# Transposing the queries and keys of an attention block with VectorE blocks and DMAs instead of TensorE

## Chip, core and metric

The kernel runs on one NeuronCore of one Trainium2 chip. The metric is device time in microseconds (us) of one execution of the whole program; the median of the runs is compared. A NeuronCore has five engines with instruction streams of their own: TensorE (PE, matrix products, its weight loads shown as PEld), VectorE (DVE), ScalarE (ACT), GpSimd (POOL) and SyncE (SP, which issues DMAs). They wait for one another through semaphores only.

## What is computed

A decoder trunk of two layers on 256 tokens of width 1024, in float32. Each layer is a mixer sub-layer (three branches in parallel, merged by gates) and a feed-forward sub-layer. Cut to what matters here:

```
z = rms_norm(x) @ w_in
c_q, c_kv, k_r, u_conv, u_pool, gate_logits = split(z)
q = (rms_norm(c_q) @ w_uq).reshape(B, S, 8, 64 + 32)     # 8 heads; the last 32 columns get rotary
k_nope = (rms_norm(c_kv) @ w_uk).reshape(B, S, 8, 64);  k_rope = rotary(k_r)   # shared by the heads
v = (rms_norm(c_kv) @ w_uv).reshape(B, S, 8, 64)
o = softmax(causal((q_nope @ k_nope.T + q_rope @ k_rope.T) / sqrt(96))) @ v    # per head
y_attn = o @ w_attn_o;  y_conv = ...;  y_pool = ...
x = x + rms_norm((g0 * y_attn + g1 * y_conv + g2 * y_pool) @ w_mix_o)
x = x + rms_norm((silu(h @ w_gate) * (h @ w_up)) @ w_down)      # h = rms_norm(x)
```

## The kernel before

**Weights as a stream of units.** The weights of a layer are cut into 135 units of at most 128x1024 numbers. SP loads unit after unit into a ring of five buffers (`raw`). Matrix products are made in a split precision: ScalarE writes a rounded copy of each unit (`w_hi`, L858), VectorE writes the rest (`w_lo = raw - w_hi`, L1185 and L1189), and TensorE makes three products for one (L438 to L440: high by high, high by low, low by high). A ring buffer is given back when TensorE has used its unit, so ScalarE and VectorE can be at most five units ahead of TensorE. One unit of a `col_group` is twelve matmuls of 512 columns.

**Order of work.** The instruction order of every engine is written by hand. TensorE goes through the groups G, A, CQ, CKV, Q, POOL, K (one unit, number 23), V (unit 24), then 24 units of gate logits (25 to 48), then the output products. Attention is threaded between the gate units: after gate unit `i` with `i` even, TensorE does `scores(i/2 - 1)`, the transposes of the probabilities of the step before, and the weighted values of the one before that (`after_gate`). So `scores(0)` stands behind the third gate unit (`i` = 2). There are 8 steps: 4 pairs of heads by 2 halves of the tokens.

**Queries and keys.** A score product wants queries and keys with the 96 dimensions of a head on the partitions. They come out of the projections with tokens on the partitions, in `q_sb` and `k_sb`. TensorE turns them with `transposes` (L512): a group is four heads of one half of the tokens, 4 transposes into one PSUM buffer `tp`, and ScalarE copies it to SBUF (`store_T`, L997) into `q_t` (in `gates`) and `k_t` (in `u_sb` and `hc`). Per layer there are 4 groups Q0 to Q3 and 4 groups K0 to K3: Q0, Q1 ahead of the K unit, Q2, Q3 ahead of the V unit (behind eight `band` matmuls of the pooling branch, L679 and L681), K0, K1 behind gate unit `i` = 0, K2, K3 behind `i` = 1. Each score product is one `pe.matmul` per head (L719), with 128 keys for the first half of the tokens and 256 for the second; the profile shows a float32 `pe.matmul` as two records.

**VectorE around it.** After the rotary of q (`rope`, L1242 to L1249) VectorE does unit 23, three convolution taps (L1264), unit 24, the rotary of k, three taps, and then `lo(u)` and three taps for each of the units 25 to 28. In the gate loop it does for each `i` the attention work (mask and maximum L1372 and L1375), `lo(29 + i)` and four taps. It does the 124 taps of a layer in one fixed order.

**GpSimd.** It computes the inverse norms (L1578, L1581) and rests from the one of c_kv until the sums over the convolution (`tile_sum`, L1625), which wait for the last tap.

**A path that exists already.** In the feed-forward sub-layer the hidden activations are transposed without TensorE: VectorE transposes 32x32 blocks (`turn`, L1488), and SP moves the blocks to their partitions with 16 DMAs a chunk (`place`, L405).

Of the kernel before, what the change touches and what calls it, by code (L numbers as in the profile page):

```python
# [44 lines left out]

BLK = 32
QUADS = P // BLK


POOL_LO = {(l, u) for l in range(LAYERS) for u in (U_FFN, U_FFN + 1)}  # L50
# [35 lines left out]
def fulls(pair, use):  # L86
# [2 lines left out]

TP = (["X0", "X1", "X2", "X3", "HC0", "HC1", "CQ0", "CQ1", "CKV0", "CKV1", "Q0", "Q1", "Q2", "Q3", "K0", "K1", "K2", "K3",
       "MT0", "MT1", *(f"{piece}{n}" for n in range(8) for piece in "PV"), "O0", "O1",
       "M0", "M1", "M2", "M3", "F0", "F1", "F2", "F3"])
TPN = {name: n for n, name in enumerate(TP)}
T_USES = len(TP)
HI_OF = [n for n in TP if n[:2] != "HC" and n[0] not in "PQKV"]
MUL_OF = [n for n in TP if n[0] in "XF"]


# [48 lines left out]
def build(nc, W, pool_w, par_d, const_d, gain_d, x_d, xc_d, pos_d, out_d):  # L149
    with ExitStack() as ctx:  # L150
        def sb(name, shape, dt=F32):
            return ctx.enter_context(nc.sbuf_tensor(name, shape, dt))

        def sem(name):
            return ctx.enter_context(nc.semaphore(name))
# [10 lines left out]
        gain = sb("gain", [P, D])  # L166
        const = sb("const", [P, NCONST])
        par = sb("par", [P, LAYERS, NPAR])
        hc = sb("hc", [P, TOK, CONV])
        sg = sb("sg", [P, TOK, 512])  # L170
        u_sb = sb("u_sb", [P, TOK, 512])
        hcT = sb("hcT", [P, CT, TAPS - 1 + SEQ])
        cacc = sb("cacc", [P, CT, SEQ])
        gates = sb("gates", [P, TOK, 3 * D])
# [24 lines left out]
        o_sb = qk_flat[:, 2048:3072].rearrange("p (t n) -> p t n", t=TOK)  # L199
        junk = qk_flat[:, 0:D]  # L200
        pooled = sg[:, :, :].rearrange("p t n -> p (t n)").rearrange("p (g n) -> p g n", g=4)


        q_t = [gates[:, hh, 2 * D:3 * D].rearrange("p (h s) -> p h s", h=4) for hh in range(2)]
        k_t = [buf[:, :, :].rearrange("p t n -> p (t n)").rearrange("p (h s) -> p h s", h=4)
               for buf in (u_sb, hc)]
        rope_a, rope_b = hc[:, 0, :], hc[:, 1, :]
        xc = hc[:, :, :].rearrange("p t n -> p (t n)").rearrange("p (c n) -> p c n", c=CT)
        sq = sg[:, :, :].rearrange("p t n -> p (t n)").rearrange("p (c n) -> p c n", c=CT)
# [62 lines left out]
        q_roped = sem("q_roped")  # L272
        k_roped = sem("k_roped")
        k_nope = sem("k_nope")
        conv_dve = sem("conv_dve")
        csum_done = sem("csum_done")
        centred = sem("centred")
# [157 lines left out]
        def _(pe):  # L435
# [23 lines left out]
            for l in range(LAYERS):  # L459
# [47 lines left out]
                def transposes(n, blocks):  # L507

                    b = n % 2
                    tp_wait(n)  # L510
                    for i, (src, rows) in enumerate(blocks):
                        mm = pe.transpose(tp[0:rows, b, i * P:(i + 1) * P], src, ident)  # L512
                    mm.then_inc(tp_full[b], 1)
# [140 lines left out]

                col_group(U_POOL, 4, 2, 512, 1, "POOL", XT)

                def q_transposes(hh):
                    for t in range(TOK):
                        if hh == 0:
                            pe.wait_ge(q_roped, l + 1)  # L660
                        transposes(TPN["Q0"] + 2 * hh + t, [(q_sb[:, t, h * QK:(h + 1) * QK], QK)
                                                            for h in range(4 * hh, 4 * hh + 4)])

                q_transposes(0)

                for t in range(TOK):
                    tp_emptied(pe, l, TPN["CKV0"] + t)
                col_group(U_K, 1, 2, 512, 0, "K", HT, kt0=H_CKV)
# [5 lines left out]
                for h in range(2):  # L674
# [6 lines left out]
                        mm = pe.matmul(misc[:, h, c + P:c + SEQ], u_sb[:, 1, g * P:(g + 1) * P],  # L681
                                       band[:, SEQ:BANDW], start=False, stop=True)
                    mm.then_inc(misc_full[h], 1)
                q_transposes(1)

                col_group(U_V, 1, 2, 512, 1, "V", HT, kt0=H_CKV)

# [8 lines left out]
                                           pw_sb[:, g * P:(g + 1) * P], pooled[:, g, :], start=True, stop=True)  # L696
                        mm.then_inc(tp_full[n % 2], 1)

                def k_transposes(n):
                    hh, t = n // 2, n % 2  # L700
                    if hh == 0:
                        pe.wait_ge(k_roped, l + 1)
                        pe.wait_ge(k_nope, l * TOK + (t + 1))
                    transposes(TPN["K0"] + n, [(k_sb[:, t, h * QK:(h + 1) * QK], QK)
                                               for h in range(4 * hh, 4 * hh + 4)])

                def scores(n):
                    hp, t = n // 2, n % 2
                    keys = (t + 1) * P
                    if n == 0 or n == 4:  # L710
                        for k in range(2):
                            tp_emptied(pe, l, TPN["K0"] + n // 2 + k)
                    if n < 2:
                        misc_emptied(pe, l, n, M_D)
                    else:
                        pe.wait_ge(exp_done, l * STEPS + n - 1)
                    for i in range(2):
                        h = 2 * hp + i
                        mm = pe.matmul(misc[:, n % 2, i * keys:(i + 1) * keys], q_t[h // 4][0:QK, h % 4, tokens(t)],  # L719
                                       k_t[h // 4][0:QK, h % 4, 0:keys], start=True, stop=True)  # L720
                    mm.then_inc(s_done, 1)

                def p_transposes(n):
# [27 lines left out]
                              ).then_inc(misc_full[0], 1)  # L751

                def attention(i):
                    if i < 2:
                        for n in range(TOK):
                            k_transposes(2 * i + n)
                    s_n, p_n, v_n = after_gate(i)
                    if s_n is not None:
                        scores(s_n)
                    if p_n is not None:  # L760
                        p_transposes(p_n)
                    if v_n is not None:
                        weighted_values(v_n)
                    if i in O_AFTER:
                        o_transposes(O_AFTER.index(i))
                    if i == MT_AFTER:
                        pool_products()
                    if i == MEAN_AFTER:
                        norm_mean()
# [72 lines left out]
        def _(act):  # L842
# [3 lines left out]
            for l in range(LAYERS):  # L846
# [143 lines left out]
                    act.activation(u_sb[:, t, :], acc[:, 2 + t, :], ACT.Copy,  # L990
                                   scale=rstd(l, R_X + t)).then_inc(free[2 + t], 1)

                def store_T(name, dst):

                    n = TPN[name]
                    tp_filled(act, l, n)
                    act.activation(dst, split3(tp[0:QK, n % 2, :], 4), ACT.Copy).then_inc(tp_free[n % 2], 1)  # L997

                def store_q(hh):
                    for t in range(TOK):  # L1000
                        store_T(f"Q{2 * hh + t}", q_t[hh][0:QK, :, tokens(t)])

                store_q(0)
                his(26, 27)
                for t in range(TOK):
                    bank(t, "K")
# [6 lines left out]
                for h in range(2):  # L1013
                    act.wait_ge(misc_full[h], l * 2 + 1)
                    act.activation(pooled[:, 2 * h:2 * h + 2, :], split3(misc[:, h, :], 2),
                                   ACT.Copy).then_inc(misc_free[h], 1)
                store_q(1)
                his(27, 28)
                for t in range(TOK):
                    bank(2 + t, "V")  # L1020
# [37 lines left out]
                for i in range(GATES):  # L1058
                    if i == MEAN_AFTER + 1:
                        conv_square()  # L1060
                    hi(U_GATE + 4 + i)
                    j = i // 4
                    if i == 3:
                        act.wait_ge(rhalf_done, (l + 1) * TOK)
                    if i % 4 == 3:
                        pair, branch, h = j % 2, j // 2, j % 2
                        for t in range(TOK):
                            bank(2 * pair + t, f"GATE{j}")
                            act.activation(gates[:, t, branch * D + 512 * h:branch * D + 512 * (h + 1)],
                                           acc[:, 2 * pair + t, :], ACT.Tanh,  # L1070
                                           scale=rhalf[:, l * TOK + t:l * TOK + t + 1]
                                           ).then_inc(free[2 * pair + t], 1)
                    if i < 2:
                        for n in range(2 * i, 2 * i + 2):
                            store_T(f"K{n}", k_t[i][0:QK, :, tokens(n % 2)])
                    s_n, p_n, _ = after_gate(i)
                    if p_n is not None:
                        store_p(p_n)
                    if s_n is not None:
                        exponentials(s_n)  # L1080
                    if i in O_AFTER:
                        half_ = O_AFTER.index(i)
                        hi_T(f"O{half_}", hT_hi[:, H_O + 2 * half_:H_O + 2 * half_ + 2, :])
                    if i == MT_AFTER:
                        for h in range(2):
                            hi_T(f"MT{h}", hT_hi[:, H_POOL + 2 * h:H_POOL + 2 * h + 2, :])
                    if i == 18:
                        act.preload_act_table(ACT.Silu)
# [61 lines left out]
        def _(dve):  # L1150
# [23 lines left out]
            for l in range(LAYERS):  # L1174
# [142 lines left out]
                    misc_emptied(dve, l, t, M_Q)  # L1317
                qr = q_sb[:, :, :].rearrange("p t (h d) -> p t h d", h=HEADS)[:, :, :, NOPE:QK]
                rope(qr, qr).then_inc(q_roped, 1)
                los(23, 24)  # L1320
                taps(3)
                los(24, 25)
                for t in range(TOK):
                    acc_freed(dve, l, 2 + t, "CKV")
# [2 lines left out]
                rope(k_sb[:, :, :].rearrange("p t (h d) -> p t h d", h=HEADS)[:, :, :, NOPE:QK],  # L1327
                     cq[:, :, k0:k0 + ROPE].unsqueeze(2)).then_inc(k_roped, 1)
                taps(3)
                for u in range(25, 29):  # L1330
                    lo(u)
                    taps(3)

                def conv_centre():

# [203 lines left out]
        def _(pool):  # L1539
# [30 lines left out]
            for l in range(LAYERS):  # L1570
# [48 lines left out]
                norm(R_CKV)  # L1619
                norm(R_CKV + 1)  # L1620

                def tile_sum(src, which):

                    halves = cprod[:, :, :]
                    pool.tensor_tensor(halves, src[:, 0:2, :], src[:, 2:4, :], ALU.add).then_inc(csum_done, 1)  # L1625
                    pool.wait_ge(csum_done, l * 4 + 2 * which + 1)
                    pool.tensor_tensor(csum[:, which, :], cprod[:, 0, :], cprod[:, 1, :], ALU.add
                                       ).then_inc(csum_done, 1)
# [136 lines left out]
```

## Time and profile before

| | us |
|---|---|
| median of 3 runs (lowest to highest) | 794.12 (794.04 to 794.16) |
| the profiled execution's own time | 794.23 |
| its span, first to last instruction | 792.4 |

| engine | busy share of the span |
|---|---|
| TensorE | 99% |
| VectorE | 72% |
| ScalarE | 54% |
| GpSimd | 10% |

The busy share is an average over the span. Matmuls are pipelined, so the time of one record is longer than the distance to the next; where a stretch of TensorE is priced, the distance from start to start counts. Start times in the rows are us from the first instruction.

### The profile page before, as it was taken

The numbers are of one execution on the slowest core, as the hardware profiler recorded it, in microseconds if no ns is written. First come the engines' busy times: TensorE is split into PE (matmuls) and PEld (weight loads), VectorE is DVE, ScalarE is ACT, GpSimd is POOL, SyncE is SP. The second block draws the span as 40 slices with busy tenths as digits, with TensorE's granted clock in tenths as the row PEclk, the third lists the DMA queues.
The fourth block names the chain that finished last, engine by engine and source line by source line (L and its number), as shares of the span: only waits on it lengthen the run. The fifth ranks groups of instructions, "written<-read, shape, count | busy, mean of one in ns | idle before, by whom it ended". The sixth has DMA issues, their size and how long they took to land.

```text
span 792.4 us, 10213 instructions
## 1 busy us (share of the span) xinstructions
PE 784.0 (99%) x3740; PEld 661.7 (84%) x3740; DVE 567.6 (72%) x814; ACT 427.6 (54%) x604; POOL 78.2 (10%) x111
## 2 busy tenths in 40 slices
PE   8999999999999999999999999999999999999997
PEld 7998888888888888888889888888888888888885
DVE  6688999879675666654476979996896755556553
ACT  6577565564564454454475666556545545445441
POOL 1620000113210000000221100002203000000000
PEclk9999999999999999999999999999999999999999
DMA  9675444536567666676355654444564676666641
GB/s 357 225 247 164 156 160 134 185 125 192 171 234 229 215 210 207 210 249 208 130 201 170 223 176 133 145 150 160 166 213 167 228 223 210 226 208 213 208 156 54
DMA packets 51729, 151.26 MB, mean 191 GB/s; under 512 B 9776, under 2 KB 14896, under 8 KB 51680
## 3 DMA queue, kind: packets, MB, share of 16 engines
q1 hardware_dynamic: 51280, 148.93, 56.6%
q0 software_dynamic: 256, 1.16, 0.4%
q8 instruction: 30, 0.49, 0.3%
q10 hardware_dynamic: 144, 0.52, 0.2%
q14 instruction: 19, 0.16, 0.1%
HBM read 143.77 MB, written 1.05 MB: 183 GB/s over the span
## 4 chain that ended last, share of the span: by engine, by line
PE 98%; DMA 1%; ACT 0%; DVE 0%; DVEq 0%; POOLq 0%; issue 0%; SPq 0%; POOL 0%; ACTq 0%
PE acc L438 28%; PE acc L440 28%; PE acc L439 28%; PE acc L557 7%; PE tp L512 3%; PE misc L719 1%; PE tp L737 1%; PE tp L524 1%; DMA gates<-x_cols 1%; PE misc L679 0%; PE tp L695 0%; PE misc L439 0%; PE misc L438 0%; PE misc L440 0%; PE misc L681 0%; ACT w_hi L858 0%
## 5 line engine op out<-in xcount | busy, mean ns | idle before, releaser
L1189 DVE TENSOR_TENSOR w_lo<-raw,w_hi 128x1024 fp32r<-128x1024 f32 (+2 forms) x246 | 299.1, 1227 | 128.3 <-ACT w_hi L858 127.6
L858 ACT ACTIVATE w_hi<-raw 128x1024 fp32r<-128x1024 f32 (+2 forms) x252 | 258.6, 1039 | 167.6 <-PE acc L440 161.1
L438 PE MATMUL acc<-w_hi,xT_hi 128*128 128x512 f32 (+2 forms) x692 | 268.2, 388 | 0.0
L440 PE MATMUL acc<-w_hi,xT_lo 128*128 128x512 f32 (+2 forms) x692 | 264.9, 383 | 0.0
L439 PE MATMUL acc<-w_lo,xT_hi 128*128 128x512 f32 (+2 forms) x692 | 264.7, 383 | 0.0
L440 PEld LDWEIGHTS acc<-w_hi,xT_lo 128*128 128x128 f32 x692 | 129.9, 188 | 24.8
L439 PEld LDWEIGHTS acc<-w_lo,xT_hi 128*128 128x128 f32 x692 | 130.0, 188 | 23.9
L438 PEld LDWEIGHTS acc<-w_hi,xT_hi 128*128 128x128 f32 x692 | 130.0, 188 | 23.6
L438 PE MATMUL acc<-w_hi,hT_hi 128*128 128x512 f32 (+1 forms) x300 | 117.3, 391 | 0.0
L440 PE MATMUL acc<-w_hi,hT_lo 128*128 128x512 f32 (+1 forms) x300 | 116.2, 387 | 0.0
L439 PE MATMUL acc<-w_lo,hT_hi 128*128 128x512 f32 (+1 forms) x300 | 116.1, 387 | 0.0
L1264 DVE SCALAR_TENSOR_TENSOR cacc<-hcT,par,cacc 128x256 f32<-128x256 f32 x240 | 101.3, 480 | 0.0
L440 PEld LDWEIGHTS acc<-w_hi,hT_lo 128*128 128x128 f32 x300 | 56.3, 188 | 11.4
L439 PEld LDWEIGHTS acc<-w_lo,hT_hi 128*128 128x128 f32 x300 | 56.4, 188 | 11.0
L438 PEld LDWEIGHTS acc<-w_hi,hT_hi 128*128 128x128 f32 x300 | 56.3, 188 | 10.9
L1578 POOL TENSOR_SCALAR mean<-ssq 128x1 f32<-128x1 f32 x23 | 8.8, 383 | 443.8 <-ACT qk L877 443.3
L1185 DVE SCALAR_TENSOR_TENSOR w_lo<-raw,par,w_hi 128x512 fp32r<-128x512 f32 (+1 forms) x30 | 24.9, 864 | 6.4 <-ACT w_hi L858 6.4
L1165 DVE TENSOR_TENSOR acc<-acc,gain 128x512 f32<-128x512 f32 x16 | 10.4, 691 | 25.6 <-ACT qk L877 22.6
L1495 DVE TENSOR_TENSOR hT_lo<-gates,hT_hi 128x512 fp32r<-128x512 f32 (+1 forms) x24 | 14.4, 640 | 19.6 <-ACT hT_hi L1105 19.6
L1045 ACT ACTIVATE qk<-tp 128x256 f32<-128x256 f32 (+1 forms) x16 | 7.9, 491 | 36.2 <-PE tp L512 36.2
L1105 ACT ACTIVATE hT_hi<-gates 128x512 fp32r<-128x512 f32 (+1 forms) x24 | 13.0, 587 | 24.8 <-DMA gates<-gates 24.8
L557 PE MATMUL acc<-w_hi,xT_hi 128*128 128x512 f32 x76 | 24.0, 397 | 1.6 <-ACT w_hi L858 1.6
(147 smaller groups left out, 638.9 us busy)
## 6 DMA issues: line engine op xcount, KB each, us to landing
raw<-weights SPq DMA_DIRECT2D x247, 512.0 KB, 3.7
raw<-weights SPq DMA_DIRECT2D x14, 384.0 KB, 3.8
gates<-gates SPq DMA_DIRECT2D x160, 32.0 KB, 2.5
raw<-weights SPq DMA_DIRECT2D x8, 288.0 KB, 4.1
gain<-gains SPq DMA_DIRECT2D x4, 512.0 KB, 6.4
x_sb<-x_rows SPq DMA_DIRECT2D x2, 512.0 KB, 9.5
out_rows<-x_sb SPq DMA_DIRECT2D x4, 256.0 KB, 2.0
const<-consts POOLq DMA_DIRECT2D x1, 896.0 KB, 7.9
```

What stands on the lines that cost most here:

```text
L438: pe.matmul(out, a_hi, b_hi, start=start, stop=False)
L439: pe.matmul(out, a_hi, b_lo, start=False, stop=False)
L440: return pe.matmul(out, a_lo, b_hi, start=False, stop=stop)
L512: mm = pe.transpose(tp[0:rows, b, i * P:(i + 1) * P], src, ident)
L557: mm = pe.matmul(b, src[:, kt, tokens(t)], w[:, s, 512 * j:512 * (j + 1)], start=kt == 0 and src is xT_hi and w is w_hi, stop=last and kt ...
L858: ins = act.activation(w_hi[:, s, first:end], raw[:, s, first:end], ACT.Copy, scale=by)
L1105: act.activation(hid_part(hT_hi, j, t), placed_for(j, t), ACT.Copy).then_inc(hid_hi, 1)
L1165: dve.tensor_tensor(acc[:, 2 * t + h, :], acc[:, 2 * t + h, :], gain[:, k], ALU.mult).then_inc(yg_done, 1)
L1185: ins = dve.scalar_tensor_tensor(out=w_lo[:, s, first:end], in0=raw[:, s, first:end], scalar=par[:, l, col:col + 1], in1=f(w_hi[:, s, firs ...
L1189: ins = dve.tensor_tensor(w_lo[:, s, 0:width], raw[:, s, 0:width], f(w_hi[:, s, 0:width]), ALU.subtract)
L1264: ins = dve.scalar_tensor_tensor(out=cacc[:, c, :], in0=src, scalar=w, in1=cacc[:, c, :], op0=ALU.mult, op1=ALU.add)
L1495: dve.tensor_tensor(hid_part(hT_lo, j, t), placed_for(j, t), f(hid_part(hT_hi, j, t)), ALU.subtract).then_inc(hid_lo, 1)
```

## The change

Queries and keys are no longer transposed by TensorE. VectorE transposes them in 32x32 blocks, three instructions for q and three for k (one for each 32 of the 96 dimensions of a head, over all heads and tokens). GpSimd's queue then issues 12 DMAs for q and 12 for k, each of 32 partitions by 512 numbers (64 KB, SBUF to SBUF), which bring block column `c` of token block `q` to partitions `32c` to `32c+31`. The keys are used where they land (`u_hc`, a joint buffer of what were `u_sb` and `hc`), in four runs of 32 columns for 128 keys; the queries land in four buffers and ScalarE copies them into `q_t` (`store_q`, 4 copies of 96x512 in place of the 8 copies of `store_T`). `scores(0)` waits for all of it. Score products over 256 keys become two of 128. VectorE's taps move: three ahead of the V unit fall away there, and the units 27 and 28 get five each.

```diff
-TP = ([... "CKV0", "CKV1", "Q0", "Q1", "Q2", "Q3", "K0", "K1", "K2", "K3",
+TP = ([... "CKV0", "CKV1",
...
+        turned_q = [gates[:, i // 2, 512 * (i % 2):512 * (i % 2 + 1)] for i in range(QK // BLK)]
+        turned_k = [gates[:, 0, D:D + 512], gates[:, 1, D:D + 512], gates[:, 0, D + 512:2 * D]]
+        placed_q = [qk_flat[:, 512 * i:512 * (i + 1)] for i in range(QUADS - 1)] + [gates[:, 1, 512:1024]]
...
@@ TensorE: q_transposes and k_transposes and their calls fall away
                 def scores(n):
-                    if n == 0 or n == 4:
-                        for k in range(2):
-                            tp_emptied(pe, l, TPN["K0"] + n // 2 + k)
+                    if n == 0:
+                        pe.wait_ge(q_stored, QUADS * (l + 1))
+                        pe.wait_ge(k_in, 16 * HEAD_MOVES * (l + 1))
...
                         h = 2 * hp + i
-                        mm = pe.matmul(misc[:, n % 2, i * keys:(i + 1) * keys], q_t[h // 4][0:QK, h % 4, tokens(t)],
-                                       k_t[h // 4][0:QK, h % 4, 0:keys], start=True, stop=True)
+                        for k in range(t + 1):
+                            mm = pe.matmul(misc[:, n % 2, i * keys + k * P:i * keys + (k + 1) * P],
+                                           q_t[0:QK, t, h, :], k_t[0:QK, :, k, h, :], start=True, stop=True)
...
@@ ScalarE: store_T and store_q(0), store_q(1) of the old form fall away
+                def store_q(q):
+                    act.wait_ge(q_in, 16 * HEAD_MOVES * (l + 1))
+                    src = placed_q[q][0:QK, :].rearrange("p (t h j) -> p t h j", t=TOK, h=HEADS)
+                    act.activation(q_t[0:QK, :, :, q * BLK:(q + 1) * BLK], src, ACT.Copy).then_inc(q_stored, 1)
...
                     if i < 2:
-                        for n in range(2 * i, 2 * i + 2):
-                            store_T(f"K{n}", k_t[i][0:QK, :, tokens(n % 2)])
+                        store_q(2 * i)
+                        store_q(2 * i + 1)
...
@@ VectorE
+                def turn_heads(src, dst, done):
+                    v = src[:, :, :].rearrange("p t (h d) -> p t h d", h=HEADS)
+                    for c in range(QK // BLK):
+                        dve.transpose(dst[c].rearrange("p (t h j) -> p t h j", t=TOK, h=HEADS),
+                                      v[:, :, :, c * BLK:(c + 1) * BLK]).then_inc(done, 1)
                 los(23, 24)
-                taps(3)
+                dve.wait_ge(q_roped, l + 1)
+                turn_heads(q_sb, turned_q, q_turned)
                 los(24, 25)
...
                 taps(3)
-                for u in range(25, 29):
+                los(25, 26)
+                taps(3)
+                los(26, 27)
+                taps(2)
+                dve.wait_ge(k_roped, l + 1)
+                dve.wait_ge(k_nope, (l + 1) * TOK)
+                turn_heads(k_sb, turned_k, k_turned)
+                for u in range(27, 29):
                     lo(u)
-                    taps(3)
+                    taps(5)
...
@@ GpSimd, behind the four norms of c_q and c_kv
+                def move_heads(src, dst, turned_, landed):
+                    pool.wait_ge(turned_, (l + 1) * (QK // BLK))
+                    for c in range(QK // BLK):
+                        for q in range(QUADS):
+                            pool.dma_start(dst(slice(BLK * c, BLK * (c + 1)), q), src[c][BLK * q:BLK * (q + 1), :]
+                                           ).then_inc(landed, 16)
+                move_heads(turned_q, lambda p, q: placed_q[q][p, :], q_turned, q_in)
+                for h in range(2):
+                    pool.wait_ge(misc_full[h], l * 2 + 1)
+                move_heads(turned_k, lambda p, q: u_hc[p, q // 2, q % 2, :], k_turned, k_in)
```

## Rows read from the trace of the kernel before

**Rows 1.** The page's busy times (us, share, instructions) and granted clock, in 40 slices.
```profile
PE 784.0 (99%) x3740; PEld 661.7 (84%) x3740; DVE 567.6 (72%) x814; ACT 427.6 (54%) x604; POOL 78.2 (10%) x111
...
PEclk9999999999999999999999999999999999999999
```

**Rows 2.** Waits of TensorE: us in total, times, longest.
```profile
PE acc L557 <- ACT w_hi L858: 1.6, 1, 1.6
```

**Rows 3.** Groups by form: count, then busy us, mean ns of one.
```profile
L512 PE MATMUL tp<-const,qk 128*96 128x128 f32 x64 | 8.3, 272 | 0.0
```

**Rows 4.** Timeline of TensorE in both layers: start us, us, what.
```profile
64.57 0.40 PE L440 MATMUL acc<-w_hi,xT_lo 128*128 128x512 f32 x1
64.80 1.04 PE L512 MATMUL tp<-const,qk 128*96 128x128 f32 x8
65.60 0.48 PE L438 MATMUL acc<-w_hi,hT_hi 128*128 128x512 f32 x1
65.91 0.39 PE L439 MATMUL acc<-w_lo,hT_hi 128*128 128x512 f32 x1
...
74.67 0.39 PE L438 MATMUL acc<-w_hi,xT_hi 128*128 128x512 f32 x1
...
77.39 1.03 PE L512 MATMUL tp<-const,qk 128*96 128x128 f32 x8
...
84.64 0.61 PE L719 MATMUL misc<-u_sb,gates 96*128 96x128 f32 x4
85.09 1.89 PE L695 MATMUL tp<-sg,pw_sb 128*128 128x256 f32 x8
...
92.28 1.03 PE L719 MATMUL misc<-u_sb,gates 96*128 96x256 f32 x4
93.15 0.38 PE L512 MATMUL tp<-const,qk 128*128 128x128 f32 x2
...
474.30 0.61 PE L719 MATMUL misc<-u_sb,gates 96*128 96x128 f32 x4
```

**Rows 5.** Timeline of VectorE, at the rotary in both layers and at a transpose.
```profile
61.39 1.41 DVE L1185 SCALAR_TENSOR_TENSOR w_lo<-raw,par,w_hi 128x512 fp32r<-128x512 f32 x2
62.71 1.27 DVE L1264 SCALAR_TENSOR_TENSOR cacc<-hcT,par,cacc 128x256 f32<-128x256 f32 x3
63.91 1.41 DVE L1185 SCALAR_TENSOR_TENSOR w_lo<-raw,par,w_hi 128x512 fp32r<-128x512 f32 x2
...
67.48 1.22 DVE L1189 TENSOR_TENSOR w_lo<-raw,w_hi 128x1024 fp32r<-128x1024 f32 x1
68.62 1.27 DVE L1264 SCALAR_TENSOR_TENSOR cacc<-hcT,par,cacc 128x256 f32<-128x256 f32 x3
...
284.35 1.30 DVE L1488 STREAM_TRANSPOSE gates<-u_sb 128x512 f32<-128x512 f32 x2
...
449.87 1.41 DVE L1185 SCALAR_TENSOR_TENSOR w_lo<-raw,par,w_hi 128x512 fp32r<-128x512 f32 x2
```

**Rows 6.** Timeline of ScalarE.
```profile
68.63 0.69 ACT L1007 ACTIVATE qk<-acc,rstd 128x512 f32<-128x512 f32 x1 [0.45 <-PE acc L440]
...
78.03 1.08 ACT L997 ACTIVATE u_sb<-tp 96x512 f32<-96x512 f32 x2 [0.57 <-PE tp L512]
```

**Rows 7.** Timeline of GpSimd and, last row, of VectorE.
```profile
16.62 0.81 POOL L1595 DMA_DIRECT2D const<-consts  x1 [15.80 <-ACT w_hi L858]
17.43 0.56 POOL L1596 DMA_DIRECT2D pos_i<-pos  x1
...
20.84 0.62 POOL L1599 DMA_DIRECT2D par<-params  x1
21.47 0.53 POOL L1600 DMA_DIRECT2D const<-consts  x1
...
52.69 1.09 POOL L1578 TENSOR_SCALAR mean<-ssq 128x1 f32<-128x1 f32 x1
...
20.76 2.36 DVE L1189 TENSOR_TENSOR w_lo<-raw,w_hi 128x1024 fp32r<-128x1024 f32 x2 [0.30 <-ACT w_hi L858]
```

**Rows 8.** DMA issues: count, KB each, median us from issue to landing.
```profile
gates<-gates SPq DMA_DIRECT2D x160, 32.0 KB, 2.5
par<-params POOLq DMA_DIRECT2D x1, 161.0 KB, 3.9
```

More of the change, by code:

```diff
@@ L47 @@
 QUADS = P // BLK
+HEAD_MOVES = QUADS * (QK // BLK)
 POOL_LO = {(l, u) for l in range(LAYERS) for u in (U_FFN, U_FFN + 1)}
@@ L88, in fulls @@
     return len([u for u in upto if pair == 0 or u not in WIDE])
-TP = (["X0", "X1", "X2", "X3", "HC0", "HC1", "CQ0", "CQ1", "CKV0", "CKV1", "Q0", "Q1", "Q2", "Q3", "K0", "K1", "K2", "K3",
+TP = (["X0", "X1", "X2", "X3", "HC0", "HC1", "CQ0", "CQ1", "CKV0", "CKV1",
        "MT0", "MT1", *(f"{piece}{n}" for n in range(8) for piece in "PV"), "O0", "O1",
@@ L96 @@
 T_USES = len(TP)
-HI_OF = [n for n in TP if n[:2] != "HC" and n[0] not in "PQKV"]
+HI_OF = [n for n in TP if n[:2] != "HC" and n[0] not in "PV"]
 MUL_OF = [n for n in TP if n[0] in "XF"]
@@ L168, in build @@
         par = sb("par", [P, LAYERS, NPAR])
-        hc = sb("hc", [P, TOK, CONV])
         sg = sb("sg", [P, TOK, 512])
-        u_sb = sb("u_sb", [P, TOK, 512])
+        u_hc = sb("u_hc", [P, 2, TOK, 512])
         hcT = sb("hcT", [P, CT, TAPS - 1 + SEQ])
@@ L201, in build @@
         pooled = sg[:, :, :].rearrange("p t n -> p (t n)").rearrange("p (g n) -> p g n", g=4)
-        q_t = [gates[:, hh, 2 * D:3 * D].rearrange("p (h s) -> p h s", h=4) for hh in range(2)]
-        k_t = [buf[:, :, :].rearrange("p t n -> p (t n)").rearrange("p (h s) -> p h s", h=4)
-               for buf in (u_sb, hc)]
+        u_sb, hc = u_hc[:, 0], u_hc[:, 1]
+        q_t = gates[:, :, 2 * D:3 * D].rearrange("p t (h s) -> p t h s", h=HEADS)
+        k_t = u_hc[:, :, :, :].rearrange("p b c (t h j) -> p (b c) t h j", t=TOK, h=HEADS)
+        turned_q = [gates[:, i // 2, 512 * (i % 2):512 * (i % 2 + 1)] for i in range(QK // BLK)]
+        turned_k = [gates[:, 0, D:D + 512], gates[:, 1, D:D + 512], gates[:, 0, D + 512:2 * D]]
+        placed_q = [qk_flat[:, 512 * i:512 * (i + 1)] for i in range(QUADS - 1)] + [gates[:, 1, 512:1024]]
         rope_a, rope_b = hc[:, 0, :], hc[:, 1, :]
@@ L274, in build @@
         k_nope = sem("k_nope")
+        q_turned = sem("q_turned")
+        k_turned = sem("k_turned")
+        q_in = sem("q_in")
+        q_stored = sem("q_stored")
+        k_in = sem("k_in")
         conv_dve = sem("conv_dve")
@@ L655, in _ @@
                 col_group(U_POOL, 4, 2, 512, 1, "POOL", XT)
[L657 to L664, printed above, removed]
                 for t in range(TOK):
@@ L683, in _ @@
                     mm.then_inc(misc_full[h], 1)
-                q_transposes(1)
                 col_group(U_V, 1, 2, 512, 1, "V", HT, kt0=H_CKV)
@@ L697, in pool_products @@
                         mm.then_inc(tp_full[n % 2], 1)
[L699 to L705, printed above, removed]
                 def scores(n):
@@ L753, in attention @@
                 def attention(i):
-                    if i < 2:
-                        for n in range(TOK):
-                            k_transposes(2 * i + n)
                     s_n, p_n, v_n = after_gate(i)
@@ L991, in _ @@
                                    scale=rstd(l, R_X + t)).then_inc(free[2 + t], 1)
[L993 to L1003, printed above, removed]
+                def store_q(q):
+                    act.wait_ge(q_in, 16 * HEAD_MOVES * (l + 1))
+                    src = placed_q[q][0:QK, :].rearrange("p (t h j) -> p t h j", t=TOK, h=HEADS)
+                    act.activation(q_t[0:QK, :, :, q * BLK:(q + 1) * BLK], src, ACT.Copy).then_inc(q_stored, 1)
                 his(26, 27)
@@ L1016, in _ @@
                                    ACT.Copy).then_inc(misc_free[h], 1)
-                store_q(1)
                 his(27, 28)
```

## The prediction

> **What bounds the kernel now.** I read the busy times first: TensorE is busy 99% of the span [rows 1]. The waits of TensorE then show one pause of 1.6 us, at the start, and nothing behind it [rows 2]. So every instruction taken from TensorE shortens the kernel by its distance to the next one, as long as nothing new keeps TensorE waiting; and every new wait counts in full. The other engines have room on average, but what counts is when the new chain VectorE, GpSimd, DMA, TensorE ends in two places, at `scores(0)` of each layer. The timelines of those stretches decide it.
>
> **What goes.** The transposes of q and k are 64 matmuls of the form 128*96 [rows 3]: 32 a layer, in four lots of eight. The lot at 64.80 ends when the next matmul starts at 65.60, and that one takes 0.31 us to its successor where 0.23 is the rule (64.57 to 64.80) [rows 4]: 0.80 + 0.08 = 0.88 us. Four lots are 3.5 us a layer, 7.0 in all. On ScalarE eight copies of 96x512 become four; a pair takes 1.08 us [rows 6] and the cost is nothing either way, since they lie beside TensorE's gate units.
>
> **What costs TensorE nothing or almost.** A score step over 256 keys takes 0.87 us for four records (92.28 to 93.15), one over 128 keys 0.45 for four (84.64 to 85.09) [rows 4]. Eight records of 128 are then 0.9, as before. Keys read in four runs of 32 have no row; bounds are nothing and, if every one of the 96 records that read keys (64 of them in the second halves) cost double, 96 x 0.11 = 10.6 us. I take nothing, since the products that read a plain run are the nearest.
>
> **When the keys are turned.** In layer 0 VectorE starts unit 23 at 61.39, with q already rotated. From there, start to start [rows 5]: unit 23 1.32 (61.39 to 62.71); three transposes of q; unit 24, the rotary of k and three taps 3.57 (63.91 to 67.48); unit 25 1.14 (67.48 to 68.62); three taps 1.19 (62.71 to 63.91); unit 26 1.14; two taps 0.80; three transposes of k. Two transposes of 128x512 take 1.30 us; with one at 0.69 that is one each 0.61, so three are 1.83. (The new ones read runs of 32 numbers at a stride of 96; the 20 old ones also pick blocks, so I take their price.) Sum: 12.8, and 0.1 for the semaphore: k is turned at 74.3, q at 64.6. ScalarE's copy of the keys, at 68.63 before [rows 6] and earlier now, isn't late. In layer 1 VectorE starts the same unit at 449.87, so q is turned at 453.1 and k at 462.8.
>
> **The train of DMAs.** Four issues on GpSimd's queue took 0.81, 0.56, 0.62 and 0.53 us [rows 7], whatever their size. I take 0.57, the mean of the last three. The twelve of q end at 64.6 + 6.8 = 71.4, ahead of the keys: hidden. The last of the keys is issued at 74.3 + 11 x 0.57 = 80.6. From issue to landing SP's copies inside SBUF take 2.5 us, GpSimd's load of 161 KB 3.9, but this with the DMA engines full [rows 8]. I take 3.5, nearer to GpSimd's own; bounds 2.5 and 3.9. The keys are in at 84.1 in layer 0 and at 462.8 + 6.3 + 3.5 = 472.6 in layer 1.
>
> The Trainium skill ("DMA: Bandwidth & Descriptors", Specifications) puts the first byte of a DMA issued from GpSimd at about 1 us and one from SP at about 0.6. By that the landing would be 2.5 + 0.4 = 2.9 us, an estimate from that page, and the sum below would end 1.2 us lower. No row here has a small GpSimd copy on idle DMA engines.
>
> **When TensorE comes.** `scores(0)` started at 84.64 and 474.30 [rows 4]. All four lots stood ahead of it: 81.1 and 470.8. So TensorE waits 3.0 us in layer 0 and 1.8 in layer 1; I add 0.2 each for the refill. The copies of q by ScalarE aren't last: q lands at 64.6 + 11 x 0.57 + 3.5 = 74.4, ScalarE comes to them about 76 (two copies stood at 78.03 [rows 6]) and the second pair follows one unit later, by 79. Behind it nothing waits longer: the waiting TensorE has ScalarE's and VectorE's units up to the ring's end.
>
> **VectorE's debt.** It gets 6 transposes, 3.7 us a layer, and TensorE asks 0.5 to 2 us earlier. At `i` = 2 VectorE comes to the mask of step 0 about 86, 1 us later against the scores than before. A gate unit needs its `w_lo` four units (4 x 2.72 us, 74.67 to 77.39 being one [rows 4]) after VectorE may start on it, and the probabilities have two gate units to be ready; both cover that debt. Without the cover (VectorE 8 us late) it would stall TensorE for the excess.
>
> **Sum.** -7.0 + 3.0 + 1.8 + 0.4 = -1.8. The profiled execution took 794.23, 0.11 above the median, so 792.4 there and **792.3** as median. Bounds of this case: issues of 0.53 and landing in 2.5 give waits of 1.5 and 0.3, sum -4.8, 789.3; issues of 0.63 (mean of all four) and landing in 3.9 give 4.1 and 2.9, sum +0.4, 794.5.
>
> **Rivals.**
>
> *The train is slow, the kernel slower.* An issue costs more than 0.57: the first row is 0.81, and a GpSimd operation on a single column took 1.09 us at 52.69, in a stretch where VectorE was working. VectorE is busy nearly without a break here. Against it: the issues at 20.84 and 21.47 lay inside two such operations (20.76 to 23.1) and took 0.62 and 0.53 [rows 7]. Each 0.1 us more adds 2 x 11 x 0.1 = 2.2; the sum is zero at 0.65 us an issue, and above that the change loses. At 0.81, q's train ends just as k is turned (74.3): -1.8 + 22 x 0.24 = +3.5, 797.6. At 1.09 q's train holds the keys up too (until 77.7; layer 1 466.2): waits 12.1 and 10.9, sum +16.4, 810.5. The Trainium skill ("SBUF — State Buffer", on the shared port pair) has the rule: GpSimd can't write descriptors while VectorE runs an operation in a two-port mode, but a `tensor_tensor` takes only the read side. By that the train isn't held, as rows 7 say; by its copy rule it would be, and no row here shows a copy.
>
> *No wait at all, the full gain.* The keys would have to land by 81.1, that is 6.8 us after being turned for 11 issues and a landing. With issues of 0.53 that leaves 1.0 for the landing, below every row. The time would be 787.1. For it speaks only that issues may overlap.
>
> *The pause costs clock.* Granted clock was full (2.4 GHz) throughout [rows 1], also over the only pause, 1.6 us [rows 2]; no row tells of 3 us. If it fell to half in each layer for one gate unit (2.72 us): +5.4, sum +3.6, 797.7. The Trainium skill ("TensorE: Matmul & The Clock Gate", Why this matters for your kernels) warns of pauses of this kind between bursts of matmuls.
>
> *Keys in runs slow the products.* +10.6 at most, sum +8.8, 802.9. No row speaks for it or against it.
>
> **Chances.** Forecast 0.47; slow train 0.33; full gain 0.07; clock 0.08; runs 0.05. A measurement here can tell about 0.2%, 1.6 us. Faster by more (below 792.5): half of the forecast, 0.25, and the full gain, with some issues below the rows: 0.37. Within: most of the rest of the forecast and the mild end of the slow train, 0.23. Slower: 0.40. The range for 8 in 10 leaves out the full gain and a train above about 0.9 us an issue (each 0.1 past 0.81 adds 2 x 2.3, as both trains count): 789 to 802; the forecast's own range is 789.3 to 794.5.
>
> **What would show it.** L512 with 128*96 gone, TensorE busy 7 us less. 24 issues a layer on GpSimd at about 0.57 us from 64.6 and from 74.3, the last landing about 84. One wait of TensorE at L719 on a DMA in each layer, 3.0 and 1.8 us: longer if the train is slow, absent if the full gain is had. Matmuls behind the wait at 0.23 us a step; 0.45 would be the clock. Six transposes of 0.69 us a layer. The prediction is wrong if the issues take more than 0.65 us or a landing much more than 3.9.

## The result, and the profile after

| | us |
|---|---|
| before, median of 5 runs (lowest to highest) | 794.12 (793.93 to 794.16) |
| changed, median of 5 runs | 796.84 (796.31 to 801.25) |
| ratio, 95% interval | 1.0051 (1.0028 to 1.0073) |
| profiled execution of the changed kernel, its span | 796.84, 795.0 |

The changed kernel is slower by 2.7 us, where 1.8 us less was forecast. Its runs also spread over 4.9 us, those of before over 0.2. The ratio is that of the means (798.12 to 794.07), which the two longest runs lift; that of the medians is 1.0034. The page's busy times and granted clock after:

```profile
PE 779.8 (98%) x3708; PEld 658.3 (83%) x3708; DVE 574.3 (72%) x826; ACT 423.8 (53%) x596; POOL 102.8 (13%) x159
...
PEclk9999999999999999999999999999999999999999
```

TensorE's busy time fell by 4.2 us only [rows 1]. Its waits after (us in total, times, longest):

```profile
PE misc L712 <- issue: 6.8, 2, 4.1
PE misc L467 <- DVE diag L1135: 1.2, 1, 1.2
PE acc L567 <- ACT w_hi L848: 0.9, 1, 0.9
```

There are two new pauses ahead of the first scores of a layer (L712 is the score product, L719 before). "issue" stands there because the profile names no instruction that released them. The only things waited for there are the stored queries and the keys' DMAs; ScalarE had stored the last queries by 79.4 us, so it was the DMAs, and experiment 1 confirms it. The other two rows are pauses in the first 9 us, and stood there before as well. The chain that ended last, in order of time, around the two places (start, us, what):

```profile
80.92 0.23 PE acc L450
81.15 4.08 issue
85.23 1.18 PE misc L712 x4
86.41 2.90 PE tp L695 x8
89.31 0.23 PE acc L448
...
473.07 0.23 PE acc L450
473.30 2.76 issue
476.06 0.68 PE misc L712 x4
476.74 1.73 PE tp L695 x8
478.47 0.23 PE acc L448
```

TensorE arrives at 81.15, as forecast (81.1), and waits 4.08 us, then 2.76 us in layer 1. Behind the first pause the same work takes longer than behind the second: 4.08 us for the scores and the pooling products against 2.41. The windows show the clock in that stretch (columns: us, busy time and count by engine, granted clock, DMA share, GB/s):

```profile
78.00:81.00 3.00, 3.00 (x14) 2.26 (x13) 3.00 (x7) 2.35 (x4) 2.58 (x6) 1.00 1.05 249
81.00:85.00 4.00, 0.15 (x1) 0.00 (x0) 4.00 (x9) 0.00 (x0) 0.00 (x0) 1.00 1.02 264
85.00:87.00 2.00, 1.77 (x6) 1.68 (x7) 1.31 (x4) 0.00 (x0) 0.00 (x0) 0.56 0.90 311
87.00:89.00 2.00, 2.00 (x8) 1.61 (x6) 1.69 (x3) 1.38 (x5) 0.00 (x0) 0.59 0.02 6
...
474.00:476.00 2.00, 0.00 (x0) 0.00 (x0) 2.00 (x5) 0.00 (x0) 0.00 (x0) 1.00 0.87 252
476.00:478.00 2.00, 1.94 (x11) 1.81 (x12) 1.97 (x5) 0.29 (x2) 0.00 (x0) 1.00 0.82 268
```

Two things are to be seen. After the pause of 4.08 us the granted clock is at half (1.2 GHz) for some 3.4 us (the means of 0.56 and 0.59 over 4 us); after 2.76 us it stays full. And the DMA engines are full from 78 to 85 us, at only 249 and 264 GB/s, where the full engines moved 399 to 422 GB/s in the trace of before (4 to 16 us). The timeline of GpSimd, whose instructions here are the issues of the copies:

```profile
64.84 1.62 POOL L1626 DMA_DIRECT2D qk<-gates  x3 [10.36 <-DVE gates L1308]
...
70.34 0.50 POOL L1626 DMA_DIRECT2D gates<-gates  x1
74.73 5.85 POOL L1626 DMA_DIRECT2D u_hc<-gates  x12 [3.89 <-DVE gates L1308]
```

The train of the keys is quicker than forecast: 5.85 us for twelve, 0.49 each (0.57 forecast). Its last copy is issued at 80.1. The lines of the copies (ns of one issue, least, median, most) and of the landing in `u_hc`:

```profile
L1626 POOL DMA_DIRECT2D u_hc<-gates x24: 496/496/498, 74.7 to 471.1; - x24
...
DMA to landing us min/median/max: 1.8/4.0/5.1
```

From 80.1 to 85.2, when TensorE goes on, are 5.1 us. So the issue is not what is slow, the landing is. VectorE's part came as priced, 12 transposes of 0.69 us; so did the score steps over 256 keys, 0.89 us for eight records of 128:

```profile
94.78 0.89 PE misc L712 x8
...
L1308 DVE STREAM_TRANSPOSE gates<-qk 128x512 f32<-128x512 f32 x12 | 7.6, 685 | 0.0
```

The sum of the profiled executions (796.84 - 794.23 = +2.6): -7.0 for the transposes, +6.8 for the pauses, +1.7 for the clock (scores 85.23 to 86.20 in place of 0.45 us, pooling products 86.20 to 88.96 in place of 1.54 [rows 4]), +0.6 behind VectorE's last entry in the chain (see the last section), and 0.5 left over, which I put down to refills of TensorE and small shifts without having traced it.

```profile
85.23 1.18 PE L712 MATMUL misc<-u_hc,gates 96*128 96x128 f32 x4 [4.08 <-issue]
86.20 3.11 PE L695 MATMUL tp<-sg,pw_sb 128*128 128x256 f32 x8
88.96 0.58 PE L448 MATMUL acc<-w_hi,xT_hi 128*128 128x512 f32 x1
```

### The profile page after: what moved, and what is told of

Same layout as the page of the kernel before. It is cut to its first block, busy times and chain, and to the rows that moved or that the text cites. A ratio compares the mean times of both kernels' runs of the same rounds, so it can differ in the third digit from the quotient of the medians.

```text
span 795.0 us, 10195 instructions
## 1 busy us (share of the span) xinstructions
PE 779.8 (98%) x3708; PEld 658.3 (83%) x3708; DVE 574.3 (72%) x826; ACT 423.8 (53%) x596; POOL 102.8 (13%) x159
## 3 DMA queue, kind: packets, MB, share of 16 engines
HBM read 143.77 MB, written 1.05 MB: 182 GB/s over the span
## 4 chain that ended last, share of the span: by engine, by line
PE 97%; issue 1%; DMA 1%; ACT 0%; DVE 0%; DVEq 0%; POOLq 0%; SPq 0%; POOL 0%; ACTq 0%
PE acc L448 28%; PE acc L450 28%; PE acc L449 28%; PE acc L567 7%; PE tp L522 2%; PE misc L712 1%; PE tp L730 1%; PE tp L534 1%; DMA gates<-x_cols 1%; PE tp L695 1%; PE misc L680 0%; PE misc L450 0%; PE misc L449 0%; PE misc L448 0%; PE misc L682 0%
```

## Experiments

All times are medians; each ratio is that of the means, to the kernel before, run on the same chip. The edits are against the changed kernel and cut to what matters; `...` marks a cut.

**1. No copies: what are the transposes worth?**

```diff
-                        pe.wait_ge(k_in, 16 * HEAD_MOVES * (l + 1))
...
-                    act.wait_ge(q_in, 16 * HEAD_MOVES * (l + 1))
...
-                move_heads(turned_q, ...)                      # GpSimd: both trains left out
...
-                move_heads(turned_k, ...)
...
+            pool.memset(gates[:, 1, 512:1024], 0.0)            # once, so that the buffer holds numbers
```

> Leaves out all 48 copies between partitions and the waits on their landing (the scores then use what lies in the buffers; one buffer is set to zero once at the start); VectorE's six transposes and ScalarE's four copies a layer stay. Theory A (the 64 matmuls are worth 7.0 us, and the loss comes only from waiting for the landing and what the wait brings): no wait at the first scores, granted clock 0.999, 787.1 us. Rival B (VectorE's new work or the split score products cost TensorE time too): 788.5 or more. The stores at the end took 0.6 us longer in the two runs with GpSimd copies looked at; if that comes from the copies it is gone here, else it adds up to 0.7.

Measured: 787.59 us, ratio 0.9915 (0.9901 to 0.9928); runs within 0.2 us. There is no pause at the first scores; layer 0:

```profile
81.23 0.45 PE misc L711 x4
```

So leaving out the 64 matmuls is worth 6.7 us (794.27 before on this chip), and VectorE's transposes, ScalarE's copies and the split score products together cost at most the 0.3 us that are missing to 7.0. Theory A holds. All of the loss is in the copies.

**2. Weight loads held back while the keys travel.**

```diff
                 for u in range(0 if l else 1, UNITS):
+                    if u == 32:
+                        sp.wait_ge(k_in, 16 * HEAD_MOVES * (l + 1))
                     load(l, u, unit_width(u))
```

> The changed kernel with SP's load of weight unit 32 (and so of all behind it) held until the keys have landed, in each layer; TensorE needs that unit some 15 us later. Theory E (the last copies land 5 us after their issue because copies and weight loads together fill the DMA engines): the last landing falls to 3.5 us or less, the waits from 4.1 and 2.8 to about 2.6 and 1.3, the clock stays full, 794.1 - 7.0 + 3.9 + 0.2 = 791 to 792.5. Rival F (the landing time is GpSimd's own and doesn't depend on the loads): landing and waits as before, 796 to 797.

Measured: 789.1 us (789.08 to 789.4), ratio 0.9937 (0.9925 to 0.9949). This one wait (two lines) turns a loss of 2.7 us into a gain of 5.1. Landing in `u_hc` and the chain in layer 0:

```profile
DMA to landing us min/median/max: 1.8/1.9/2.2
...
81.16 0.86 issue
82.01 0.68 PE misc L714 x4
```

The train is the same (0.50 us an issue, from 74.7), but a copy lands in 1.9 us in place of 4.0. The pause is 0.86 us in layer 0 and gone in layer 1, less than theory E said, since it allowed 3.5 us for the landing; the time is below its 791 to 792.5 for the same reason. Theory E holds, F falls. The queues' packets, MB and shares of the 16 DMA engines from 78 to 81 us, with loads held:

```profile
q0 software_dynamic: 191, 0.39, 60.6%
```

and in the changed kernel:

```profile
q0 software_dynamic: 219, 0.46, 67.5%
q1 hardware_dynamic: 87, 0.29, 37.6%
```

and before, from 78 to 84 us, where the weight loads were alone:

```profile
q1 hardware_dynamic: 298, 1.09, 58.2%
```

Six copies were issued in those 3 us: 0.606 x 3 / 6 = 0.30 us of all engines for 64 KB. At one copy in 0.5 us the train alone takes 0.6 of the engines, and the weight loads took 0.58 of them in this place before. Together that is more than there is, so copies queue up behind loads, up to 5 us. A copy itself holds the engines no longer beside the loads than without them (0.675 x 3 us for 0.46 MB, 4.4 us per MB, against 0.606 x 3 for 0.39, 4.7): it waits for its turn and isn't moved more slowly. But per MB a copy costs more than a load (0.582 x 6 us for 1.09 MB, 3.2), which is a part of why the full engines move so little.

The mean shares explain only a part of the size: 0.18 too much over the 5.9 us of the train leaves 1.1 us of work behind, and the landing grew by 2.1 us in the median and 2.9 at most (from 1.9 and 2.2 to 4.0 and 5.1). The engines had been full from 70 to 74 us already (share 1.05), with the last copies of the queries beside the loads, and a load comes as one piece of 512 KB, by the figure above 1.7 us of all engines, an estimate. How much each of these adds wasn't separated.

**3. Keys turned earlier.**

```diff
-                taps(3)
                 los(25, 26)
                 taps(3)
-                los(26, 27)
-                taps(2)
                 dve.wait_ge(k_roped, l + 1)
                 dve.wait_ge(k_nope, (l + 1) * TOK)
                 turn_heads(k_sb, turned_k, k_turned)
+                los(26, 27)
+                taps(5)
```

> The changed kernel with VectorE's three transposes of the keys moved ahead of unit 26 and of three taps: they end about 3.1 us earlier (74.1 to about 71). GpSimd's train for the queries ends at 70.8, so the keys' train starts about 71.2 in place of 74.7, 3.5 us earlier. Theory A (the moment of the turn sets the wait): waits fall from 4.1 and 2.8 to about 0.6 and 0, the clock stays full, 794.1 - 7.0 + 0.6 + 0.2 = 787.9, at most 789.5. Rival B (the landing of the last copy is set by the DMA engines being full until then and doesn't move with the issue): waits stay above 2, 791 to 795.

Measured: 794.38 us, but from 791.28 to 801.78 over 12 runs; ratio 1.0015 (0.9993 to 1.0036). Neither expectation is met alone. The two long waits are 2.45 us in layer 0 and 1.04 in layer 1. The train starts 2.95 us earlier (71.78), TensorE goes on only 1.46 us earlier (83.77): half of the head start is lost again to the landing, whose median is 4.4 us, the longest 6.5. B is nearer. And the clock fell after the pause of only 2.45 us (not after that of 1.04):

```profile
DMA to landing us min/median/max: 3.5/4.4/6.5
...
81.32 2.45 issue
83.77 1.19 PE misc L712 x4
84.96 2.90 PE tp L695 x8
...
85.00:87.00 2.00, 2.00 (x6) 1.55 (x6) 1.97 (x6) 0.20 (x1) 0.00 (x0) 0.50 0.70 248
```

The mean clock of the runs goes with their time: 0.997 to 0.999 in those of 791.3 and 792.5 us, 0.992 and 0.990 in those of 800.0 and 801.8.

**4. The pause filled with work.**

```diff
                     if n == 0:
+                        misc_emptied(pe, l, 0, M_D)
+                        for _ in range(5):        # 3 in the second kernel
+                            pe.matmul(misc[:, 0, 0:512], ident, const[:, K_BAND:K_BAND + 512], start=True, stop=True)
                         pe.wait_ge(q_stored, QUADS * (l + 1))
                         pe.wait_ge(k_in, 16 * HEAD_MOVES * (l + 1))
```

> The changed kernel with five extra matmuls of 512 columns (ten records, about 2.1 us, result overwritten) ahead of TensorE's wait for queries and keys, in each layer: they fit into the pauses of 4.1 and 2.8 us and leave 2.0 and 0.7 of them. Theory C (the pause itself lets the clock fall, which costs 1.7 us in the profiled run and more in the runs of 799 and 801): 795.1 us, granted clock 0.999, and a spread below 0.5 us. Rival D (the low clock in that stretch has another cause than the pause): 796 to 801 as before, granted clock 0.99 to 0.996.

Measured: 796.98 us (796.51 to 797.95), ratio 1.0038 (1.0026 to 1.005), granted clock 0.998 to 0.999 in all five runs. The clock did what theory C said; the time (795.1 expected) and the spread (1.4 us in place of 0.5) didn't. Layer 0:

```profile
81.58 4.29 PE misc L705 x10
85.87 0.58 issue
```

The ten records take 4.29 us, double of what I allowed, and in layer 1 (pause 2.76) they hold TensorE up by 1.5 us themselves. So with three matmuls again:

> The changed kernel with three extra matmuls of 512 columns (six records of 0.43 us as measured with five of them, 2.6 us in all) ahead of the wait, in each layer; they fit into the pauses of 4.1 and 2.8 us. Theory C (the pause lets the clock fall): granted clock 0.999, 796.8 less 1.7 = 795.1, spread below 1 us. Rival D (another cause): 796 to 801 and clock 0.990 to 0.996 as in the changed kernel.

Measured: 795.25 us, ratio 1.0013 (1.0004 to 1.0022). Ten of eleven runs lie between 794.48 and 795.57 with a clock of 0.998 or 0.999; one is at 798.2 with 0.996, so the spread is 3.7 us where below 1 was expected. The chain in layer 0 and layer 1:

```profile
81.09 2.58 PE misc L705 x6
83.66 1.48 issue
85.14 0.68 PE misc L715 x4
85.83 1.73 PE tp L695 x8
...
471.60 2.58 PE misc L705 x6
474.18 0.51 issue
474.69 0.68 PE misc L715 x4
```

The keys come as late as in the changed kernel, but the work behind them takes 2.4 us, not 4.1. So 1.6 us of the loss, and most of the spread, come from the clock, and the clock falls when TensorE stands still: the same kernel with work in the pause keeps 0.998 or more in 15 of 16 runs. Theory C holds. The one run at 0.996 may be a fall after the 1.5 us of pause that was left; it wasn't profiled, so that isn't shown.

**5. Keys issued by SP.**

```diff
+                    if u == 32:                                # in SP's stream, ahead of the load
+                        sp.wait_ge(k_turned, (l + 1) * (QK // BLK))
+                        for h in range(2):
+                            sp.wait_ge(misc_full[h], l * 2 + 1)
+                        for c in range(QK // BLK):
+                            for q in range(QUADS):
+                                sp.dma_start(u_hc[BLK * c:BLK * (c + 1), q // 2, q % 2, :],
+                                             turned_k[c][BLK * q:BLK * (q + 1), :]).then_inc(k_in, 16)
...
-                move_heads(turned_k, ...)                      # GpSimd: the keys' train left out
```

> The changed kernel with the 12 copies of the keys issued by SP, ahead of its load of unit 32, in place of GpSimd. SP issues in order, so the loads behind stand back as in the kernel with held loads. SP's own copies take 0.6 us an issue, so the train is 7.2 us in place of 5.9. Theory E (what matters is that the loads stand back): landing 2 us after the last issue at 74.7 + 11 x 0.6 = 81.3, so 83.3, wait 2.1 in layer 0 and about 0.9 in layer 1, 790.5 to 792 us, clock seldom below full. Rival H (GpSimd's queue is at fault for the late landing, in whatever company): landing and waits clearly shorter than with held loads and GpSimd (0.9 and 0), below 789.1.

Measured: 792.48 us (790.79 to 792.75), ratio 0.9969 (0.9959 to 0.9979). SP's train, the chain in layer 0, and the granted clock behind the pause:

```profile
74.22 7.57 SPq L425 DMA_DIRECT2D u_hc<-gates  x12
...
81.19 2.10 issue
83.29 0.68 PE misc L720 x4
...
85.00:87.00 2.00, 2.00 (x6) 1.60 (x5) 1.97 (x6) 0.33 (x2) 0.00 (x0) 0.50 0.97 358
```

SP's issues take 0.63 us, GpSimd's 0.49; the landing is 2.0 us here and 1.9 with GpSimd and held loads. With the loads standing back both queues land alike, so GpSimd's queue isn't at fault and H falls; it is in fact the better one for this train. With the longer train the pause is 2.10 us, as expected (0.89 in layer 1), and the clock fell even after that in the profiled run: it was still full for the score products and fell during the pooling products, which took 2.56 us in place of 1.73. That it would be seldom below full was wrong, and the median lies above the 790.5 to 792 expected. The nine runs stand in two groups, 790.8 to 791.3 with mean clocks of 0.998 to 1.0, and 792.5 to 792.8 with 0.996 in four of five; I take the groups for runs without and with the fall, though only one run of the upper group was profiled.

**6. Half of the change: queries only.** VectorE and GpSimd turn q; TensorE transposes k as before, and ScalarE stores it in the new order.

```diff
-                        pe.wait_ge(k_in, 16 * HEAD_MOVES * (l + 1))
+                        for k in range(4):
+                            tp_emptied(pe, l, TPN["K0"] + k)
...
+                    if i < 2:
+                        for n in range(TOK):
+                            k_transposes(2 * i + n)
...
-                move_heads(turned_k, ...)                      # GpSimd: the keys' train left out
```

> Half of the change: queries by VectorE and GpSimd's 12 copies, keys transposed by TensorE as before (ScalarE stores them in the order of the new layout, on top of its four copies of queries). Theory A: 32 of 64 transposes gone, 3.5 us, and the queries land before they are needed: no new wait, 790.6 us, spread below 0.5 us. Rival G (the queries' train hurts by itself, through weights or ScalarE's copies that come late): 792 or more.

Measured: 790.92 us (790.8 to 791.15), ratio 0.9957 (0.9943 to 0.9971). 3.3 us faster, no new pause: theory A. The queries' half of the change is sound as it is: some 10 us lie between their last issue and the first scores. The whole loss is with the keys.

**7. Both repairs: keys turned earlier and loads held (from unit 31).** The edits of 2 and 3 together.

> Both repairs: keys turned before unit 26 (their train starts at 71.8) and SP's load of unit 31 and all behind it held until the keys have landed. Theory E (weight loads and copies fill the DMA engines together): landing of the last copy 2 us, at 79.6, ahead of TensorE's arrival at 81.1; no wait in either layer; 0.9 us better than with the loads held alone (789.1), so 788.2, spread below 0.5 us, granted clock 0.999. Rival F (with the loads held the turn no longer matters): 789.1.

Measured: 788.03 us (787.86 to 788.17), ratio 0.992 (0.9907 to 0.9934). The pause is gone in both layers; layer 0:

```profile
81.18 0.45 PE misc L714 x4
81.62 1.73 PE tp L697 x8
```

This version beats before by 6.2 us and the changed kernel by 8.8. The edit that won only half of its head start in experiment 3 takes a further 1.1 us off once the loads stand back (here from one unit earlier on, which wasn't tried by itself).

## Why the prediction was wrong

**Where it landed.** The measured 796.84 lies inside the range for 8 in 10 (789 to 802) and outside the forecast's own (789.3 to 794.5); the change moved the time the other way.

**Right.** TensorE is the bound and the transposes are worth 3.5 us a layer (6.7 of 7.0 in all, experiment 1). TensorE's arrival at 81.1, the moments when VectorE is ready (74.2 against 74.3), the train's length (80.1 against 80.6 for the last issue), the hidden queries (though they were in only at 76.3, not 74.4), VectorE's debt and the cost of keys in runs (0.89 us a step): all as worked out. VectorE's two-input operations didn't slow the issues: 0.496 us median while VectorE was busy without a break. The Trainium skill ("SBUF — State Buffer", Who interferes with whom) says that an operation with two inputs in SBUF, outside the two-port modes, takes only the read side of the port pair that VectorE shares with GpSimd, and infers that writing descriptors needs the write side. The trace agrees. One reading was incomplete: TensorE had two pauses before, 1.6 and 1.2 us, not one, both at the start; nothing hung on it.

**The step that failed** is "From issue to landing ... I take 3.5 ... bounds 2.5 and 3.9". It measured 5.1 and 4.9 us for the last copy of a layer. I took the bounds from single transfers and treated the landing as a latency. It is a queue: twelve copies at 0.30 us of all 16 engines each, one every 0.5 us, beside weight loads that already took 0.58 of the engines. I had read the DMA share of this stretch and not added the train to it. The two landings were 3.0 us longer than forecast together; last issues 0.5 us earlier against TensorE's arrival in each layer hid 1.0 of it, which was luck, so the two pauses came out 2.0 us longer (6.8 against 4.8). That alone turns -1.8 into +0.2. With 4.08 and 2.76 us the pauses are still within what the forecast's upper bound allowed (4.1 and 2.9, sum +0.4), by the wrong two terms; what carried the time beyond 794.5 stands in the next paragraph. With the loads away the landing is 1.9 us (experiment 2), below my lower bound; so the range missed on both sides, by what the neighbours do. The Trainium skill's rule that DMAs from all issuing engines run on the same 16 engines and interleave ("DMA: Bandwidth & Descriptors", Issuing engines are not separate DMA queues) is what this trace shows, and it belonged in the sum.

**A rival that came true on top.** The sum had the clock at nothing, though it forecast pauses of 3.0 and 1.8 us and no row told of such a pause. "The pause costs clock" had 0.08, by itself, and was priced at 2.7 us a layer. It isn't independent of the first error (the counts of runs in the last section). It cost 1.7 us in layer 0 of the profiled execution and nothing in layer 1, and makes most of the spread of 4.9 us. Together with 0.6 us at the end, which nothing in the trace of before hinted at, the terms carry the forecast -1.8 to +2.6.

**The slow side was right for the wrong reason.** I gave 0.33 to slower issues. The issues were faster than in every row of before.

## What to carry over

A transfer inserted beside a stream of loads isn't priced by a latency row: work out what the whole train takes of the DMA engines, add it to their share in that stretch, and if the sum is over 1 the landing grows beyond any row of a single transfer. Look then for a load that can wait: here two lines that hold back loads needed some 15 us later were worth 7.7 us. And if TensorE is the bound, price a new pause at its length plus the slow stretch that may follow (here 1.7 us, in some runs), and take a spread of the runs as a sign that a pause lets the clock fall in some.

## What was unexpected of the hardware

**Short pauses and the clock.** The granted clock fell to half after pauses of 4.08, 2.45 and 2.10 us and stayed full after one of 2.76 us, and one kernel (experiment 3) gave 791 to 802 us. The runs' mean clocks show how often (the pause is the longest behind the first 9 us in the kernel's profiled run): 0.996 or lower in 5 of 5 runs of the changed kernel with 4.08 us, in 9 of 12 with 2.45 us, in 4 of 9 with 2.10, in 1 of 11 with 1.48, and in none with 0.86 or less. So the longer the pause, the likelier the fall, but the length alone doesn't decide it. The Trainium skill ("TensorE: Matmul & The Clock Gate", Why this matters for your kernels) warns of pauses between bursts of matmuls. The trace agrees; here some shorter than those it names sufficed.

**0.6 us at the end.** From VectorE's last entry in the chain to the end of the span are 3.1 us before (789.28 to 792.4) and 3.7 after (791.26 to 795.0). It is 3.7 to 3.8 in all six kernels in which GpSimd issues both trains (48 copies), and 3.1 to 3.2 where it issues one train (experiments 5 and 6) or none (experiment 1). It goes with the number of GpSimd's copies, and not evenly; the mechanism stays open.

**What stays open.** Four unprofiled runs (799.5 and 801.3 us of the changed kernel, 800.0 and 801.8 in experiment 3) have mean clocks of 0.992 or 0.990. That is more low clock than a stretch of 3.4 us behind each of the two pauses would give, and where it lay wasn't seen. How the clock's fall depends on the moment of the pause wasn't tried. Nor was whether fewer, larger copies would take less of the DMA engines.
